# Expert matmuls of a hybrid decoder step: weights as the stationary operand, token blocks of 96 as the moving one

## The chip, the cores and the metric

One core of a Trainium2 chip runs the whole kernel. The metric is device time in microseconds (us) of one execution, median of several; lower is better. Engines are named as in the profile: PE is TensorE's matmul, PEld its loading of the stationary operand, DVE is VectorE, ACT ScalarE, POOL GpSimd, SP the queue that issues the weight transfers.

## The reference

One step of a two-layer decoder for 256 prompt tokens and 8 x 4 sample tokens, 288 rows of width 1024. Layer 0 is a Mamba-2 / sliding-window attention mixer and a dense SwiGLU; layer 1 is an RWKV-7 mixer and a mixture of experts, which is the part that matters here:

```python
def _swiglu(h, wg, wu, wd):
    return (jax.nn.silu(h @ wg) * (h @ wu)) @ wd

def _moe(h, router, wg, wu, wd):                    # 8 experts, D = 1024, EXPERT_FF = 2816
    logits = jnp.einsum('bld,de->ble', h, router)
    top_v, top_i = lax.top_k(logits, 2)
    gates = jax.nn.softmax(top_v, axis=-1)
    combine = jnp.einsum('blk,blke->ble', gates, jax.nn.one_hot(top_i, 8))
    y = jnp.zeros(h.shape, f32)
    for e in range(8):
        y = y + combine[..., e:e + 1] * _swiglu(h, wg[e], wu[e], wd[e])
    return y
```

All values are float32. The 288 rows have 576 (row, expert) pairs. With the reference's own inputs (its default seed) the eight experts get 70, 77, 68, 84, 76, 64, 60 and 77 rows.

## The kernel before, in words

Layer 0 and the RWKV mixer take roughly the first half of the span and are not touched. In the expert part the rows of one expert are gathered into a block of at most 128 slots; a block is one `job(j)`. An expert with more rows than slots gets another block, up to `NJ`. The router's counts decide how many jobs there are, and `jobi` carries the number to every engine; jobs 1 to the last but one run in a hardware loop, job 0 and the last are written out beside it. With the counts above there are eight jobs.

A job walks over 2816 = `FC` x 256 inner columns in `FC` = 11 chunks. For one chunk SP loads 3 MB (`load_part`, L825): 128 x 4096 floats of gate and up weights ("gu") and 128 x 2048 of down weights ("dn"), into a ring of four slots.

The products are wanted to nearly float32 accuracy from single-pass matmuls, so every operand is split in two: a head (ACT rounds it to fp32r, `heads` and `token_heads`, L1418, L1423, L1428) and a rest (DVE subtracts the head from the value, `rests` and `token_rests`, L2143, L2149, L2156). A product is then head x head + head x rest + rest x head, three matmuls that add into the same PSUM bank.

On PE, all matmuls of the helper `mm` stand at L2342. For chunk c the queue has:

- `up(c)`: the tokens are the stationary operand (`hsel`, 128 x 128 for each of the eight k-tiles of D), and the weights stream past as 512 moving columns, gate 256 and up 256. That is 8 x 3 = 24 matmuls. The result has tokens on partitions.
- `down(c - 2)`: 12 matmuls, the activation stationary (`actTm`, tile `actT_split` in the profile) and 512 moving columns of down weights.
- `turn(c - 1)`: since the activation must have inner columns on partitions, two 128 x 128 transposes (L3127) turn it, from PSUM bank 2 or 7.

ACT and DVE make the activation of a chunk from PSUM: Silu of the gate half (ACT, L1486), product with the up half (DVE, L2291), and after the transposes its head (ACT, L1493) and rest (DVE, L2307). Each engine runs its queue strictly in program order. At the end of a job the next block's rows, fetched by POOL from DRAM (`next_rows`), are turned by eight transposes (`turn_tokens`, L3080), and ACT copies the job's result out (`rows_out`, L1435, L1436), which POOL stores. The last job also brings all rows back to their tokens and adds them to the residual.

The lines that matter most in the code are these three, in `up`:

```python
mm(ps[:, c % 2, :], hh[:, k, :], wh[:, k, :], k == 0, False)
mm(ps[:, c % 2, :], hh[:, k, :], wr[:, k, :], False, False)
ins = mm(ps[:, c % 2, :], hr[:, k, :], wh[:, k, :], False, k == KT - 1)
```

(the second argument is the stationary operand, the third the moving one).

Of the kernel before, what the change touches and what calls it, by code (L numbers as in the profile page):

```python
# [5 lines left out]
F32 = mybir.dt.float32  # L6
# [26 lines left out]
FC = FF // 256  # L33
C_DECAY = float(np.exp(-0.5))
# [95 lines left out]
def decoder_trunk(nc, a, out):  # L130
    with ExitStack() as ctx:
# [219 lines left out]
        actTm = [[actTm_[:, (2 * i + u) * 256:(2 * i + u + 1) * 256] for u in range(2)] for i in range(2)]  # L351
# [6 lines left out]
        NJ = NE + 4  # L358
        flags, posn, erow, jrow = [moe_area(16) for _ in range(4)]
        ohx, tmpx = [moe_area(64).rearrange("p (x i) -> p x i", x=4) for _ in range(2)]  # L360
# [11 lines left out]
        DOWN_BANKS = [0, 1, 2, 7, 5, 6, 3, 4]  # L372
        moe_rows = nc.dram_tensor("moe_rows", ((NJ + 1) * P, D), F32, kind="Internal").ap()
        moe_back = nc.dram_tensor("moe_back", (NJ * P, D), F32, kind="Internal").ap()

# [13 lines left out]
        def turned(c):  # L389

            return ps[:, 2 if c % 2 == 0 else 7, 0:256]
# [368 lines left out]
        def _(sp):  # L760
# [110 lines left out]
            jl = sp.value_load(jobi[0:1, 4:5], min_val=NE - 1, max_val=NJ - 1)  # L871
# [12 lines left out]
        def _(pool):  # L884
# [15 lines left out]
            for n, t in enumerate(X_ORDER):  # L900
# [11 lines left out]
                if n == 4:  # L912
                    pool.wait_ge(sem("pool_cleared"), 2)
                    pool.dma_start(moe_rows.rearrange("(b p) n -> p b n", p=P), zeros.unsqueeze(1).broadcast_to([P, NJ + 1, D]))\
                        .then_inc(sem("rows_zeroed"), 16)
                    pool.dma_start(moe_back[(NE - 1) * P:, :].rearrange("(b p) n -> p b n", p=P),
                                   zeros.unsqueeze(1).broadcast_to([P, NJ - NE + 1, D])).then_inc(sem("rows_zeroed"), 16)
# [91 lines left out]
            jl = pool.value_load(jobi[0:1, 4:5], min_val=NE - 1, max_val=NJ - 1)  # L1009
            def next_rows(j):  # L1010
                pool.wait_ge(sem("gather_full"), 2 * j + 2)
                pool.dma_start(xtok, moe_rows[bass.ds(j * P + P, P), :]).then_inc(sem("xtok_loaded"), 16)

            def store_rows(j):
                pool.wait_ge(sem("y_out"), j)
                pool.dma_start(moe_back[bass.ds(j * P - P, P), :], ysb).then_inc(sem("back_stored"), 16)
                pool.wait_ge(sem("back_stored"), 16 * j)
                pool.sem_inc(sem("ysb_free"), 1)

            next_rows(0)  # L1020
            with pool.Fori(1, jl) as j:
                next_rows(j)
                store_rows(j)
            pool.wait_ge(sem("gather_full"), 2 * jl + 2)
            store_rows(jl)
            for c, (t0, n) in enumerate(TOK):
                if c == 2:
                    pool.wait_ge(sem("pair_summed"), 1)
                    pool.wait_ge(sem("y_final"), 2)
                for a_ in range(2):  # L1030
                    pool.indirect_dma_start(pair[a_][c][0:n, :], None, moe_back,
                                            bass.IndirectOffsetOnAxis(ap=rows_in[0:n, 3 * a_ + c:3 * a_ + c + 1], axis=0))\
                        .then_inc(sem(f"pair_loaded{c}"), 16)


        @block.scalar
        def _(act):
# [387 lines left out]
            def token_heads(j, u):  # L1425

                act.wait_ge(sem("gather_full"), 2 * j + 1 + u)
                A(hsel[0][:, 4 * u:4 * u + 4, :], ps[:, 5 + u, :].rearrange("p (k c) -> p k c", k=4), ACT.Copy)\  # L1428
                    .then_inc(sem("hsel_head"), 1)

            def rows_out(j):
# [3 lines left out]
                A(ysb[:, 0:512], ps[:, 3, :], ACT.Copy)  # L1435
                A(ysb[:, 512:1024], ps[:, 4, :], ACT.Copy).then_inc(sem("y_out"), 1)  # L1436
# [29 lines left out]
            def job(j, first, last=False):  # L1466
# [4 lines left out]
                else:  # L1471
                    heads(j, 0, "gu", range(4))
                    rows_out(j)
                    heads(j, 1, "gu", range(2))
                for c in range(FC + 1):
                    if last and c == 5:
                        act.wait_ge(sem("gather_full"), 2 * j + 3)
                        A(sel_last, ps[:, 5, 0:T], ACT.Copy).then_inc(sem("hsel_head"), 1)
                    if last and c in (4, 6, 9):
                        pair_scale((4, 6, 9).index(c))  # L1480
                    if c < FC:
                        act.wait_ge(sem("gu_full"), FC * j + c + 1)
                        act.sem_inc(sem(f"gu_slot_free{c % MS}"), 1)
# [5 lines left out]
                    if c == FC - 1:  # L1489
                        heads(j, c, "dn", range(1))  # L1490
                    if c:
                        act.wait_ge(sem("tr_full"), FC * j + c)
                        A(actTm[(c - 1) % 2][0], turned(c - 1), ACT.Copy).then_inc(sem("tr_head"), 1)  # L1493
                    if c + 2 < FC:
                        heads(j, c + 2, "gu", range(1, 2))
                    if c < FC - 1:
                        heads(j, c, "dn", range(1))
                if last:
                    act.wait_ge(sem("pair_summed"), 2)
                    act.wait_ge(sem("gather_full"), 2 * j + 10)  # L1500
                    A(ysb[:, 0:512], ps[:, 3, :], ACT.Copy).then_inc(sem("y_out"), 1)
# [6 lines left out]
            jl = act.value_load(jobi[0:1, 4:5], min_val=NE - 1, max_val=NJ - 1)  # L1508
# [6 lines left out]
        def _(dve):  # L1515
# [636 lines left out]
            def token_rests(j, u):  # L2152
# [3 lines left out]
                V.tensor_tensor(hsel[1][:, hv, :], ps[:, 5 + u, :].rearrange("p (k c) -> p k c", k=4),  # L2156
# [1126 lines left out]
```

## Time and profile before

| | |
|---|---|
| median of 3 executions | 1634.34 us (1631.61 to 1641.16) |
| the profiled execution, its own time | 1637.31 us |
| its span, first to last instruction | 1634.3 us |
| PE busy / DVE busy / ACT busy | 1590.1 / 1137.9 / 896.8 us |
| mean granted TensorE clock | 0.987 of full |
| matmuls | 10856, and as many loads of a stationary operand |
| HBM read | 379.09 MB, 248 GB/s over the span |

The busy time of PE counts a matmul from its issue to its last result, and neighbours overlap, so a mean of 390 ns is no price of one more matmul; the price is the distance between the starts of neighbours in the timeline. The same holds for PEld.

### The profile page before, as it was taken

To read this page: it belongs to the slowest core of one execution; us is meant where nothing else is said; L and a number is where in the kernel's file an instruction comes from. 1 tells how busy PE (TensorE), PEld (TensorE's weight loads), DVE (VectorE), ACT (ScalarE), POOL (GpSimd) and SP (SyncE) were. 2 spreads that over 40 slices of the span, in tenths; PEclk is the share of its full clock that TensorE was granted. 3 is DMA by queue.
4 is the path that set the end of the run, shared out by engine and by line. 5 is a ranking of instruction groups with operands and counts; after the bars stand their busy time and mean duration, and the time that the engine had idled before them with its cause. 6 is when DMAs were issued, how large, how long until landed. Compare 5 with 4: busy or idle time off the path is not lost.

```text
span 1634.3 us, 27320 instructions
## 1 busy us (share of the span) xinstructions
PE 1590.1 (97%) x10856; PEld 1309.2 (80%) x10856; DVE 1137.9 (70%) x1476; ACT 896.8 (55%) x1190; POOL 123.3 (8%) x180
## 2 busy tenths in 40 slices
PE   9999999999999999899999999999999999999999
PEld 7766687999998777778767878888787887878787
DVE  4663741677766753335468889797988979798897
ACT  3362541544325353343436777676777767687774
POOL 1104000000000003220222000000000000000100
PEclk9999889999999999998999999999999999999999
DMA  8923533544423240000449999797989979798993
GB/s 334 407 94 124 207 130 123 220 187 170 175 81 119 103 155 1 3 3 2 187 165 395 380 376 412 316 427 305 425 350 376 409 312 426 303 425 347 384 423 121
DMA packets 41103, 404.74 MB, mean 248 GB/s; under 512 B 4784, under 2 KB 5072, under 8 KB 11664
## 3 DMA queue, kind: packets, MB, share of 16 engines
q1 hardware_dynamic: 34336, 372.25, 56.6%
q0 software_dynamic: 6672, 31.14, 4.7%
q8 instruction: 70, 1.15, 0.3%
q14 instruction: 25, 0.20, 0.0%
HBM read 379.09 MB, written 26.30 MB: 248 GB/s over the span
## 4 chain that ended last, share of the span: by engine, by line
PE 88%; DVE 5%; ACT 2%; DMA 2%; issue 2%; POOL 0%; DVEq 0%; ACTq 0%; SPq 0%; POOLq 0%
PE ps L2342 85%; DMA ring<-in_moe_w 1%; PE ps L3127 1%; DMA arena<-in_moe_w 1%; DVE rest_ring L2149 1%; PE ps L2809 1%; PE ps L2750 1%; DVE arena L1688 0%; ACT arena L1270 0%; DVE arena L1701 0%; ACT arena L1283 0%; PE ps L3080 0%; PE ps L2544 0%; DVE h L2057 0%; DVE arena L1776 0%
## 5 line engine op out<-in xcount | busy, mean ns | idle before, releaser
L2342 PE MATMUL ps<-head,hsel 128*128 128x512 f32 x1408 | 457.5, 396 | 2.8 <-DVE rest_ring L2149 2.8
L2342 PEld LDWEIGHTS ps<-head,hsel 128*128 128x128 f32 x1408 | 264.3, 188 | 61.5 <-DVE rest_ring L2149 7.8
L2149 DVE TENSOR_TENSOR rest_ring<-ring,head 128x2048 fp32r<-128x2048 f32 x128 | 291.0, 2284 | 14.4 <-ACT head L1423 14.3
L2342 PE MATMUL ps<-arena,ring 128*128 128x288 f32 (+9 forms) x1408 | 256.6, 347 | 1.3 <-ACT arena L1276 1.2
L1423 ACT ACTIVATE head<-ring 128x2048 fp32r<-128x2048 f32 x128 | 243.1, 1912 | 24.9 <-DMA ring<-in_moe_w 24.9
L2342 PEld LDWEIGHTS ps<-arena,ring 128*128 128x128 f32 (+4 forms) x1408 | 199.5, 189 | 53.1 <-issue 7.7
L2342 PE MATMUL ps<-rest_ring,hsel 128*128 128x512 f32 x512 | 199.6, 390 | 0.0
L2342 PE MATMUL ps<-head,actT_split 128*128 128x512 f32 x512 | 169.1, 394 | 9.0 <-issue 6.3
L2342 PE MATMUL ps<-rest_arena,head 128*128 128x288 f32 x704 | 174.8, 296 | 0.0
L2342 PE MATMUL ps<-rest_arena,rest_ring 128*128 128x288 f32 x528 | 155.5, 294 | 0.0
L2342 PE MATMUL ps<-h,ring 128*128 128x288 f32 (+2 forms) x624 | 133.6, 370 | 3.7 <-ACT h L1332 1.9
L2342 PEld LDWEIGHTS ps<-h,ring 128*128 128x128 f32 (+2 forms) x624 | 99.6, 176 | 37.6 <-issue 10.7
L2342 PEld LDWEIGHTS ps<-head,actT_split 128*128 128x128 f32 x512 | 96.1, 188 | 33.3 <-issue 9.1
L2342 PEld LDWEIGHTS ps<-rest_arena,head 128*128 128x128 f32 x704 | 122.5, 188 | 0.1
L2143 DVE TENSOR_TENSOR rest_ring<-ring,head 128x2048 fp32r<-128x2048 f32 x48 | 109.7, 2285 | 9.7 <-ACT head L1418 9.7
L2149 DVE TENSOR_TENSOR rest_arena<-arena,head 128x1024 fp32r<-128x1024 f32 (+1 forms) x64 | 110.3, 1750 | 3.7 <-ACT head L1423 3.5
L2342 PEld LDWEIGHTS ps<-rest_ring,hsel 128*128 128x128 f32 x512 | 96.4, 188 | 18.0
L2342 PE MATMUL ps<-arena 64*64 64x64 f32 (+13 forms) x1514 | 96.9, 266 | 9.9 <-DVE arena L1721 4.0
L2342 PE MATMUL ps<-hsel,head 128*128 128x288 f32 x352 | 103.8, 295 | 0.0
L1599 DVE TENSOR_TENSOR x<-x,ps 128x288 f32<-128x288 f32 x110 | 48.2, 452 | 77.6 <-PE ps L2342 77.3
L1423 ACT ACTIVATE head<-arena 128x1024 fp32r<-128x1024 f32 (+1 forms) x64 | 92.4, 1485 | 15.9 <-DMA arena<-in_moe_w 15.6
L2342 PE MATMUL ps<-rest_ring,actT_split 128*128 128x512 f32 x256 | 99.7, 389 | 0.0
(387 smaller groups left out, 2283.1 us busy)
## 6 DMA issues: line engine op xcount, KB each, us to landing
ring<-in_moe_w SPq DMA_DIRECT2D x64, 2048.0 KB, 12.4
ring<-in_moe_w SPq DMA_DIRECT2D x64, 1024.0 KB, 8.3
arena<-in_moe_w SPq DMA_DIRECT2D x24, 2048.0 KB, 11.6
arena<-in_moe_w SPq DMA_DIRECT2D x24, 1024.0 KB, 6.6
ring<-in_ffn_w SPq DMA_DIRECT2D x11, 2048.0 KB, 7.4
ring<-in_ffn_w SPq DMA_DIRECT2D x11, 1024.0 KB, 4.8
moe_rows<-arena POOLq DMA_DIRECT2D x1, 6656.0 KB, 34.0
ring<-in_w_in SPq DMA_DIRECT2D x2, 3072.0 KB, 12.8
```

Of the source, the lines that this page charges most:

```text
L1423: A(mhead[c % 2][:, o:o + w], mslot[s][:, o:o + w], ACT.Copy).then_inc(sem("gu_head"), 1)
L1599: V.tensor_tensor(x[:, m, :], x[:, m, :], bank(g)[:, 0:T], ALU.add).then_inc(freesem(g), 1)
L2143: V.tensor_tensor(mrest[s][:, GU:SLOT], mslot[s][:, GU:SLOT], down_head(c).bitcast(F32), ALU.subtract).then_inc(sem("dn_split"), 1)
L2149: V.tensor_tensor(mrest[s][:, o:o + w], mslot[s][:, o:o + w], mhead[c % 2][:, o:o + w].bitcast(F32), ALU.subtract).then_inc(sem("gu_split" ...
L2342: return nc.tensor.matmul(o, l, r, start=start, stop=stop, skip_group_check=skip)
L2750: ins = nc.tensor.transpose(b[0:rows, i * P:(i + 1) * P], src[:, 4 * hf + i, t0:t0 + rows], ident)
L2809: ins = nc.tensor.transpose(b[:, n * P:(n + 1) * P], Mi[gg % 2][:, h0:h0 + 2, :].rearrange("p h t -> p (h t)"), ident)
L3127: ins = nc.tensor.transpose(turned(c)[:, u * P:(u + 1) * P], actm[c % 2][:, u * P:(u + 1) * P], ident)
```

## The change

A block has `SL` = 96 slots instead of 128, and up to 13 blocks are foreseen (`NJ`). In `up(c)` the operands change places: each 128 x 128 piece of the gate or up weights is stationary and the tokens stream. The 96 head columns and 96 rest columns of a k-tile lie side by side in `hsel`, so that a piece of the weights' head is loaded once for 192 moving columns (head x head and head x rest), and a piece of the weights' rest once for the 96 head columns. The two sums stand apart in PSUM; ACT copies one to SBUF, DVE adds the other to it, and Silu, product, head and rest are then made of 192 wide tiles in SBUF. The result has inner columns on partitions already, so `turn` is gone. `down` is as before with a 96 wide stationary operand. Two PSUM banks for each of two chunks take the place of one, in banks 0 to 3; down uses 4 and 5, token blocks 6 and 7. POOL's order of loads and stores is written out by chunk, and ACT makes the first piece of the next job's chunk 0 a little earlier. What SP loads is the same.

```diff
+SL = 96
...
-        hsel = [hsel_[:, i * 1024:(i + 1) * 1024].rearrange("p (k c) -> p k c", k=KT) for i in range(2)]
+        hsel = hsel_[:, 0:2 * KT * SL].rearrange("p (k a c) -> p k a c", k=KT, a=2)
...
-        sgm = moe_area(256)
-        actm = [moe_area(256) for _ in range(2)]
+        sgm = [moe_area(2 * SL) for _ in range(2)]
+        gsum = [moe_area(4 * SL) for _ in range(2)]
...
-        NJ = NE + 4
+        NJ = NE + 5
...
-        DOWN_BANKS = [0, 1, 2, 7, 5, 6, 3, 4]
+        GU_BANKS, DOWN, TOKB = (0, 2), 4, 6
+        FINAL_BANKS = [0, 1, 2, 3, 6, 7, 4, 5]
...
-        def turned(c):
-            return ps[:, 2 if c % 2 == 0 else 7, 0:256]
+        def gu_banks(c):
+            b = GU_BANKS[c % 2]
+            return ps[:, b:b + 2, 0:4 * SL].rearrange("p b (i a s) -> p b i a s", i=2, a=2)
+        def sums4(c):
+            return gsum[c % 2].rearrange("p (b i s) -> p b i s", b=2, i=2)
...
+            def act_silu(j, c):
+                act.wait_ge(sem("gu_free"), FC * j + c + 3)
+                A(sgm[c % 2], gsum[c % 2][:, 0:2 * SL], ACT.Silu).then_inc(sem("sums_then_silu"), 1)
+            def act_head(j, c):
+                act.wait_ge(sem("actm_ready"), FC * j + c + 1)
...
+                A(actTm[c % 2][0], sgm[c % 2], ACT.Copy).then_inc(sem("moe_act_head"), 1)
...
-                        act.wait_ge(sem("gu_free"), FC * j + c + 2)
-                        A(sgm, ps[:, c % 2, 0:256], ACT.Silu).then_inc(sem("silu_ready"), 1)
+                    A(sums4(c), gu_banks(c)[:, :, :, 1, :], ACT.Copy).then_inc(sem("sums_then_silu"), 1)
...
-                    if c:
-                        act.wait_ge(sem("tr_full"), FC * j + c)
-                        A(actTm[(c - 1) % 2][0], turned(c - 1), ACT.Copy).then_inc(sem("tr_head"), 1)
+                    act_silu(j, c)
...
+                    if c == FC - 1 and not last:
+                        heads(j + 1, 0, "gu", range(0, 1))
+                    act_head(j, c)
...
+            def act_sums(j, c):
+                dve.wait_ge(sem("sums_then_silu"), 2 * FC * j + 2 * c + 1)
+                V.tensor_tensor(sums4(c), gu_banks(c)[:, :, :, 0, :], sums4(c), ALU.add).then_inc(sem("gu_free"), 1)
+            def act_product(j, c):
+                dve.wait_ge(sem("sums_then_silu"), 2 * FC * j + 2 * c + 2)
+                V.tensor_tensor(sgm[c % 2], sgm[c % 2], gsum[c % 2][:, 2 * SL:4 * SL], ALU.mult).then_inc(sem("actm_ready"), 1)
+            def act_rest(j, c):
+                dve.wait_ge(sem("moe_act_head"), FC * j + c + 1)
+                V.tensor_tensor(actTm[c % 2][1], sgm[c % 2], actTm[c % 2][0].bitcast(F32), ALU.subtract)\
+                    .then_inc(sem("moe_act_rest"), 1)
...
-                        V.tensor_tensor(actm[c % 2], sgm, ps[:, c % 2, 256:512], ALU.mult).then_inc(sem("gu_free"), 1)
...
-                        V.tensor_tensor(hd[1], turned(c - 1), hd[0].bitcast(F32), ALU.subtract).then_inc(sem("tr_free"), 1)
...
                 def up(c):
...
-                        mm(ps[:, c % 2, :], hh[:, k, :], wh[:, k, :], k == 0, False)
-                        mm(ps[:, c % 2, :], hh[:, k, :], wr[:, k, :], False, False)
-                        ins = mm(ps[:, c % 2, :], hr[:, k, :], wh[:, k, :], False, k == KT - 1)
+                        for i in range(4):
+                            cols_ = slice(i * P, (i + 1) * P)
+                            both = sums[:, i // 2, i % 2]
+                            if k == KT - 1:
+                                mm(both[:, 0], wr[:, k, cols_], hsel[:, k, 0, :], False, False, skip=True)
+                            ins = mm(both, wh[:, k, cols_], hsel[:, k], k == 0 and i % 2 == 0, k == KT - 1, skip=True)
+                            if k < KT - 1:
+                                mm(both[:, 0], wr[:, k, cols_], hsel[:, k, 0, :], False, False, skip=True)
...
-                def turn(c):
-                    pe.wait_ge(sem("gu_free"), FC * j + c + 3)
-                    pe.wait_ge(sem("tr_free"), FC * j + c + (1 if c else 2))
-                    for u in range(2):
-                        ins = nc.tensor.transpose(turned(c)[:, u * P:(u + 1) * P], actm[c % 2][:, u * P:(u + 1) * P], ident)
-                    ins.then_inc(sem("tr_full"), 1)
...
-                    pe.wait_ge(sem("tr_free"), FC * j + c + 3)
+                    pe.wait_ge(sem("moe_act_rest"), FC * j + c + 1)
...
-                        mm(ps[:, 3 + hf, :], ah[:, us], wh[:, u, cols_], begins, False)
-                        mm(ps[:, 3 + hf, :], ah[:, us], wr[:, u, cols_], False, False)
-                        ins = mm(ps[:, 3 + hf, :], an[:, us], wh[:, u, cols_], False, ends)
+                        mm(ps[0:SL, DOWN + hf, :], ah[:, us], wh[:, u, cols_], begins, False)
+                        mm(ps[0:SL, DOWN + hf, :], ah[:, us], wr[:, u, cols_], False, False)
+                        ins = mm(ps[0:SL, DOWN + hf, :], an[:, us], wh[:, u, cols_], False, ends)
```


What this makes of PE's queue, at the end of `up(2)`, `down(0)` and the start of `up(3)` in the first written-out job. Before:

```order
L2342 MATMUL ps<-head,actT_split 128x512 x2
L2342 MATMUL ps<-rest_arena,actT_split 128x512
L2342 MATMUL ps<-head,actT_split 128x512
L3127 MATMUL ps<-cst,moe 128x128 x2
L2342 MATMUL ps<-head,hsel 128x512
L2342 MATMUL ps<-rest_ring,hsel 128x512
L2342 MATMUL ps<-head,hsel 128x512 x2
L2342 MATMUL ps<-rest_ring,hsel 128x512
```

and after (the four pieces of a k-tile read alike; `hsel,head` with 192 columns is a weights' head piece, `rest_ring` with 96 a weights' rest piece):

```order
L2377 MATMUL ps<-rest_arena,actT_split 96x512
L2377 MATMUL ps<-head,actT_split 96x512 x2
L2377 MATMUL ps<-rest_arena,actT_split 96x512
L2377 MATMUL ps<-head,actT_split 96x512 x2
L2377 MATMUL ps<-rest_arena,actT_split 96x512
L2377 MATMUL ps<-head,actT_split 96x512
L2377 MATMUL ps<-hsel,head 128x192
L2377 MATMUL ps<-hsel,rest_ring 128x96
L2377 MATMUL ps<-hsel,head 128x192
L2377 MATMUL ps<-hsel,rest_ring 128x96
```

The two transposes between `down` and `up` are gone, `down` has the same matmuls with 96 stationary columns, and a k-tile of `up` has eight matmuls in place of three: 64 in a chunk in place of 24.

DVE's queue, middle of a job (`moe` is the area of the activation tiles, 128x2048 is a rest of the weights). Before:

```order
L2291 TENSOR_TENSOR moe<-moe,ps 128x256
L2143 TENSOR_TENSOR rest_ring<-ring,head 128x2048
L2149 TENSOR_TENSOR rest_arena<-arena,head 128x2048
L2307 TENSOR_TENSOR actT_split<-ps,actT_split 128x256
L2149 TENSOR_TENSOR rest_arena<-arena,head 128x2048
L2291 TENSOR_TENSOR moe<-moe,ps 128x256
```

and after:

```order
L2196 TENSOR_TENSOR moe<-moe 128x192
L2178 TENSOR_TENSOR rest_ring<-ring,head 128x2048
L2201 TENSOR_TENSOR actT_split<-moe,actT_split 128x192
L2178 TENSOR_TENSOR rest_ring<-ring,head 128x2048
L2191 TENSOR_TENSOR moe<-ps,moe 128x384
L2172 TENSOR_TENSOR rest_ring<-ring,head 128x2048
```

The weights' rests keep their number and size; beside them stand three operations of a chunk (384, 192 and 192 wide) in place of two of 256.

## Rows read from the trace of the kernel before

**Rows 1.** The page: busy time; chain that ended last, by engine and by line

```profile
PE 1590.1 (97%) x10856; PEld 1309.2 (80%) x10856; DVE 1137.9 (70%) x1476; ACT 896.8 (55%) x1190; POOL 123.3 (8%) x180
...
PE 88%; DVE 5%; ACT 2%; DMA 2%; issue 2%; POOL 0%; DVEq 0%; ACTq 0%; SPq 0%; POOLq 0%
PE ps L2342 85%; DMA ring<-in_moe_w 1%; PE ps L3127 1%; DMA arena<-in_moe_w 1%; DVE rest_ring L2149 1%; PE ps L2809 1%; PE ps L2750 1%; DVE arena L1688 0%; ACT arena L1270 0%; DVE arena L1701 0%; ACT arena L1283 0%; PE ps L3080 0%; PE ps L2544 0%; DVE h L2057 0%; DVE arena L1776 0%
```

**Rows 2.** Windows: first job; a middle job; six chunks of it; last job; tail

```profile
core 0: us, PE busy (x) PEld busy (x) DVE busy (x) ACT busy (x) POOL busy (x), PEclk, DMA share, GB/s
858.30:954.80 96.50, 94.26 (x427) 77.16 (x427) 80.41 (x86) 65.93 (x58) 12.48 (x8) 1.00 0.91 373
1145.84:1241.44 95.60, 94.41 (x427) 76.94 (x426) 82.40 (x60) 70.25 (x61) 1.07 (x2) 1.00 0.91 373
1175.66:1226.26 50.60, 50.60 (x231) 41.57 (x230) 44.14 (x31) 35.38 (x30) 0.00 (x0) 1.00 0.89 365
1528.74:1617.60 88.86, 87.33 (x398) 70.88 (x397) 83.22 (x66) 65.69 (x55) 12.12 (x7) 1.00 0.84 350
1617.60:1634.30 16.70, 13.56 (x65) 10.57 (x63) 7.92 (x15) 3.44 (x5) 0.00 (x0) 1.00 0.19 71
```

**Rows 3.** Timeline of PE (start us, us, instruction, idle before), chunk of a middle job

```profile
1178.06 0.39 PE L2342 MATMUL ps<-rest_arena,hsel 128*128 128x512 f32 x1
1178.29 0.62 PE L2342 MATMUL ps<-head,hsel 128*128 128x512 f32 x2
1178.74 0.39 PE L2342 MATMUL ps<-rest_arena,hsel 128*128 128x512 f32 x1
...
1181.46 0.39 PE L2342 MATMUL ps<-rest_ring,actT_split 128*128 128x512 f32 x1
1181.69 0.62 PE L2342 MATMUL ps<-third_head,actT_split 128*128 128x512 f32 x2
1182.14 0.39 PE L2342 MATMUL ps<-rest_ring,actT_split 128*128 128x512 f32 x1
```

**Rows 4.** Timeline of PE, token transposes at that job's end

```profile
1234.99 1.04 PE L3080 MATMUL ps<-cst,moe 128*128 128x128 f32 x8
```

**Rows 5.** Timeline of PE, dense layer 0, 288 moving columns

```profile
430.02 0.29 PE L2342 MATMUL ps<-rest_arena,rest_ring 128*128 128x288 f32 x1
430.15 0.29 PE L2342 MATMUL ps<-rest_arena,head 128*128 128x288 f32 x1
430.28 0.29 PE L2342 MATMUL ps<-hsel,head 128*128 128x288 f32 x1
430.42 0.29 PE L2342 MATMUL ps<-rest_arena,rest_ring 128*128 128x288 f32 x1
```

**Rows 6.** Timeline of PEld where the array had stood idle, middle job

```profile
1154.72 0.19 PEld L2342 LDWEIGHTS ps<-head,hsel 128*128 128x128 f32 x1 [0.82 <-DVE rest_ring L2149]
1154.83 0.19 PEld L2342 LDWEIGHTS ps<-rest_ring,hsel 128*128 128x128 f32 x1
```

**Rows 7.** Timeline of PE, same place

```profile
1154.72 0.50 PE L2342 MATMUL ps<-head,hsel 128*128 128x512 f32 x1 [0.40 <-DVE rest_ring L2149]
1155.06 0.40 PE L2342 MATMUL ps<-rest_ring,hsel 128*128 128x512 f32 x1
```

**Rows 8.** Timeline of PEld, 1 moving column, before the experts

```profile
843.30 0.74 PEld L2342 LDWEIGHTS ps<-cst,arena 128*128 128x128 f32 x6 [0.86 <-DVE arena L1543]
```

**Rows 9.** Timeline of PEld, 64 moving columns, RWKV part

```profile
667.53 0.97 PEld L2342 LDWEIGHTS ps<-arena,ring 128*128 128x128 f32 x8
```

**Rows 10.** PEld by form (busy us, mean ns, idle before), widths 128, 64, 32

```profile
L2342 PEld LDWEIGHTS ps<-head,hsel 128*128 128x128 f32 x1408 | 264.3, 188 | 61.5 <-DVE rest_ring L2149 7.8
L2342 PEld LDWEIGHTS ps<-arena,ring 128*128 128x128 f32 x896 | 164.5, 192 | 49.0 <-issue 5.3 <-ACT arena L1276 1.7 <-DVE arena L2092 0.8
...
L2342 PEld LDWEIGHTS ps<-ring 64*64 64x64 f32 x1280 | 26.9, 133 | 17.1 <-issue 17.1
L3127 PEld LDWEIGHTS ps<-cst,moe 128*128 128x128 f32 x176 | 24.1, 140 | 10.4
...
L2342 PEld LDWEIGHTS ps<-ring 32*32 32x32 f32 x96 | 4.0, 107 | 1.6 <-issue 1.5
```

**Rows 11.** Groups of DVE by form, middle job

```profile
L2149 DVE TENSOR_TENSOR rest_ring<-ring,head 128x2048 fp32r<-128x2048 f32 x16 | 36.4, 2284 | 0.5 <-ACT head L1423 0.5
...
L2291 DVE TENSOR_TENSOR moe<-moe,ps 128x256 f32<-128x256 f32 x11 | 4.6, 420 | 8.8 <-ACT moe L1486 8.8
...
L2156 DVE TENSOR_TENSOR hsel<-ps,hsel 128x512 fp32r<-128x512 f32 x2 | 1.3, 682 | 0.0
```

**Rows 12.** Groups of ACT by form, middle job

```profile
L1423 ACT ACTIVATE head<-ring 128x2048 fp32r<-128x2048 f32 x16 | 30.4, 1912 | 1.0 <-DMA ring<-in_moe_w 1.0
...
L1486 ACT ACTIVATE moe<-ps 128x256 f32<-128x256 f32 x11 | 4.2, 385 | 15.7 <-PE ps L2342 15.7
...
L1435 ACT ACTIVATE moe<-ps 128x512 f32<-128x512 f32 x1 | 0.6, 600 | 1.1 <-PE ps L2342 1.1
```

**Rows 13.** Windows: many small matmuls; a stretch with a throttled clock

```profile
680.00:700.00 20.00, 17.87 (x547) 15.74 (x546) 8.05 (x18) 6.33 (x18) 5.10 (x8) 1.00 0.02 5
757.70:771.30 13.60, 13.60 (x106) 10.96 (x103) 7.46 (x13) 5.78 (x15) 0.00 (x0) 0.50 0.00 1
```

More of the change, by code:

```diff
@@ L1008, in _, with pair_rows @@
             pool.wait_ge(sem("jobs_ready"), 1)
-            jl = pool.value_load(jobi[0:1, 4:5], min_val=NE - 1, max_val=NJ - 1)
+            jl = pool.value_load(jobi[0:1, 5:6], min_val=NE - 1, max_val=NJ - 1)
             def next_rows(j):
                 pool.wait_ge(sem("gather_full"), 2 * j + 2)
[L1012 to L1029, printed above, removed]
+                pool.dma_start(xtok[0:SL], moe_rows[bass.ds(j * SL + SL, SL), :]).then_inc(sem("xtok_loaded"), 16)
+            def pair_rows(c):
+                n = TOK[c][1]
                 for a_ in range(2):
@@ L1033, in _, with job @@
                         .then_inc(sem(f"pair_loaded{c}"), 16)
+            def job(j, first, last=False):
+                if not last:
+                    next_rows(j)
+                for c in range(FC):
+                    if c == 0 and not first:
+                        pool.wait_ge(sem("y_out"), j)
+                        pool.dma_start(moe_back[bass.ds(j * SL - SL, SL), :], ysb[0:SL]).then_inc(sem("back_stored"), 16)
+                    if c == 1 and not first:
+                        pool.wait_ge(sem("back_stored"), 16 * j)
+                        pool.wait_ge(sem("gather_full"), 2 * j + 2)
+                        pool.sem_inc(sem("ysb_free"), 1)
+                    if last and c == 1:
+                        pair_rows(0)
+                        pair_rows(1)
+                    if last and c == 7:
+                        pool.wait_ge(sem("pair_summed"), 1)
+                        pool.wait_ge(sem("y_final"), 2)
+                        pair_rows(2)
+            job(0, True)
+            with pool.Fori(1, jl) as j:
+                job(j, False)
+            job(jl, False, last=True)
         @block.scalar
@@ L1500, in job @@
                     act.wait_ge(sem("gather_full"), 2 * j + 10)
-                    A(ysb[:, 0:512], ps[:, 3, :], ACT.Copy).then_inc(sem("y_out"), 1)
+                    A(ysb[0:SL, 0:512], ps[0:SL, DOWN, :], ACT.Copy).then_inc(sem("y_out"), 1)
                     return
@@ L2284, in job @@
                     rests(j, 0, "gu", range(4))
-                    rests(j, 1, "gu", range(0, 1))
-                for c in range(FC + 1):
-                    if c < FC:
-                        dve.wait_ge(sem("silu_ready"), FC * j + c + 1)
-                        if c >= 2:
-                            dve.wait_ge(sem("tr_full"), FC * j + c - 1)
-                        V.tensor_tensor(actm[c % 2], sgm, ps[:, c % 2, 256:512], ALU.mult).then_inc(sem("gu_free"), 1)
+                    rests(j, 1, "gu", range(2))
+                for c in range(FC):
+                    act_sums(j, c)
                     if last and c in (2, 3):
@@ L2297, in job @@
                         pair_add(j, c // 2 - 3, c % 2)
-                    if c == 0 and not first:
-                        rests(j, 1, "gu", range(1, 2))
-                    if 1 <= c <= FC - 2:
+                    if c:
                         rests(j, c - 1, "dn", range(1))
+                    act_product(j, c)
                     if c + 2 < FC:
                         rests(j, c + 2, "gu", range(0, 1))
-                    if c:
-                        dve.wait_ge(sem("tr_head"), FC * j + c)
-                        hd = actTm[(c - 1) % 2]
-                        V.tensor_tensor(hd[1], turned(c - 1), hd[0].bitcast(F32), ALU.subtract).then_inc(sem("tr_free"), 1)
+                    if c == FC - 1:
+                        rests(j, c, "dn", range(1))
+                    act_rest(j, c)
                     if c + 2 < FC:
                         rests(j, c + 2, "gu", range(1, 2))
-                    if c == FC - 2:
-                        rests(j, c, "dn", range(1))
-                rests(j, FC - 1, "dn", range(1))
                 if last:
@@ L3155, in job @@
                         down(c - 2)
-                    if 1 <= c < FC:
-                        turn(c - 1)
                     if c == FC - 1:
-                        turn(c)
                         for u in range(0 if last else 2):
```

110 lines of the change are left out of this document (55 added, 55 removed).

## The prediction

> **What bounds the kernel now.** I read the page first: PE is busy for 97% of the span, and the chain of work that ended last runs for 85% of it over one line, the matmul helper L2342 [rows 1]. Then the windows by stage. The first expert job takes 96.50 us, a middle one 95.60, and six neighbouring chunks of a middle job take 50.60 us, 8.43 us each, with PE busy in all of it, DVE in 44.14 us and ACT in 35.38 [rows 2]. So inside a job PE alone sets the pace.
>
> What a matmul costs PE is read from the distance of starts in the timeline. Three matmuls of 512 moving columns lie between 1178.06 and 1178.74, and between 1181.46 and 1182.14: 0.227 us each, in `up` and in `down` [rows 3]. The eight token transposes last 1.04 us together, one 0.27, so 0.77 / 7 = 0.11 each [rows 4]; the two of `turn` are of the same shape. A chunk is then 36 x 0.227 + 2 x 0.11 = 8.39 us, and 8.43 are seen. With 288 moving columns three matmuls take 0.40 us, 0.133 each [rows 5]. The two prices give a line: 0.42 ns a column (the granted clock is 1.00, the 2.4 GHz level) and 12 ns that do not depend on columns.
>
> Now the other half of an instruction pair, the load of the stationary operand, which today hides under a matmul of 213 ns of streaming. It shows itself where the array had stood idle: after a wait of 0.82 us one load starts at 1154.72 and the next at 1154.83, 0.11 us later [rows 6]; the matmul between them lasts 0.50 us where its neighbours last 0.39 to 0.40 [rows 7], because it had to wait those 0.11 us for its operand. Where the moving side is short, the load is all that is left: six pairs with **one** moving column have loads that span 0.74 us, one 0.19, so 0.55 / 5 = 0.11 us each [rows 8]; eight pairs with 64 moving columns span 0.97 us, 0.78 / 7 = 0.111 each [rows 9]. One and 64 columns cost the same, so the time is the larger of load and stream, not their sum. Those are fp32 operands; whether fp32r loads faster is told by the groups: 188 ns against 192 for a 128 wide load, while 64 wide ones take 133 and 32 wide 107 [rows 10]. Width sets it, and the load of the weights' type is as long as the fp32 one. **A 128 wide load costs about 0.11 us, whatever moves.**
>
> **The change part by part.**
>
> *`up`.* 24 matmuls of 0.227 us, 5.45 us, leave. 64 arrive: 32 with 192 moving columns, 32 with 96. By columns this is less work (9216 in place of 12288), but by the line above they would stream for only 0.092 and 0.052 us, both below the 0.11 of a load, and each of them has a load of its own. I take 0.112 us for each, the value of the rows with short moving sides. 64 x 0.112 = 7.17 us: **+1.72 us a chunk**. The bounds: 0.108, if load follows load as after the idle array (6.91 us), and 0.121, if the 12 ns that fp32r pays between neighbours do not hide and come on top of a load (7.74 us).
>
> *`turn`.* Two transposes leave: -0.22 us a chunk.
>
> *`down`.* Still 12 matmuls of 512 moving columns; a 96 wide load hides as a 128 wide one does. 2.72 us, no change.
>
> Chunk: 8.43 + 1.72 - 0.22 = 9.93 us. 88 chunks (8 jobs x 11): **+132 us**, between +110 and +182.
>
> *DVE.* Before, three rests of 2.28 and two operations of 0.42: 7.7 us. After, three rests (6.85), the 384 wide add, between the 0.42 of 256 and the 0.68 of 512 columns, say 0.55, and two of 192 at no more than 0.42 [rows 11]: at most 8.2 us. *ACT*: three heads of 1.91, a 384 wide copy below the 0.60 of 512, two of 192 below the 0.39 of 256 [rows 12]: at most 7.1 us. Both lie beside 9.93 us of PE and cost nothing. The new chain sums, Silu, product, head, rest must be done one chunk later, since `down(c)` stands behind `up(c + 2)`: five operations of about 2.3 us and two weight rests between them against 7.2 us of `up`. That is cover enough; with a PE chunk under 8.2 us it would not be.
>
> *Waits that go.* A middle job takes 95.60 us: 11 x 8.43 are 92.8, eight token transposes 0.9, and 2 us are waits for rests of the next job's weights and restarts. The first job has 2.9 us of them by the same sum [rows 2]; for the last, whose queue holds other transposes too, I count 2 as for a middle one: 7 x 2 + 2.9 = 17 us. DVE needs 8.2 us for a chunk that takes PE 9.93, so it arrives at the end of a job with a lead. I take 12 of them as gone; 0 to 17 are the bounds. The same slack makes the weight transfers idle more: 3.15 MB in 9.93 us is 317 GB/s where 373 are seen.
>
> *Small things.* Gathering, job ends and token transposes work on 96 in place of 128 columns (a tenth of a microsecond a job); POOL's new order has nothing queued behind it that PE waits for, its loads and stores of rows having most of a job's time. The last rows after the last `up` (16.7 us) [rows 2] keep their twenty-four `down` matmuls. Nothing is put down for these. Layer 0 and RWKV are untouched.
>
> Sum: 132 - 12 = +120 us on the profiled execution's 1637.3 us, 1757; the median of the runs lies 3 us lower, so **1754 us**.
>
> **The rivals.**
>
> *The 12 ns stay on top of every load* (0.121 us): nothing in rows 6 to 9 shows them there, but no row has fp32r operands with a short moving side in a series. +51 us: 1805 us. Chance 15%.
>
> *Loads hide after all, and the change is not slower.* The place is the pair load and matmul in `up`; it decides at 0.089 us a pair, where 64 pairs, 2.72 us of `down` and the 0.04 that 8.43 stands over 8.39 make today's 8.43 again. If loads overlapped each other or were shared by neighbours, the line's 0.092 and 0.052 us would give 4.6 us for `up`, a PE chunk of 7.3, and DVE's 8.2 us would become the bound: 88 x (8.2 - 8.43) = -20, **1614 us**. Against it stand the 0.11 us of rows 6 to 9, for it only that each piece is used once, so that the engine is free to fetch far ahead. The Trainium skill speaks for it: "TensorE: Matmul & The Clock Gate", section on the back-to-back issue gap, has 81 ns as the sustained distance of load and matmul pairs at 128 columns, an estimate of 64 x 0.081 = 5.2 us for `up`, and the same DVE bound. The trace does not agree with that for these types, with 0.11 us at 1 and at 64 columns; the same page's section on weight-path modes gives its fast load only to operands that are not fp32, and whether fp32r counts as such it does not say. Chance 7%.
>
> *PE's clock falls.* In `up` the array would stream for about two thirds of the time (0.144 of 0.224 us by the line). From 757.70 to 771.30 the granted clock was 0.50, the 1.2 GHz level, with PE busy throughout; from 680 to 700, with 547 small matmuls, it stayed at 1.00 [rows 13]. At 1.2 GHz a chunk would take twice its time: +9.9 us each, +290 us if a third of the chunks ran so, 2045 us. Chance 2%.
>
> *More jobs.* If an expert had over 96 rows, a ninth job would cost 11 x 9.93 + 1 = 110 us: 1862 us. The fullest expert has 84. Chance 1%.
>
> **How the numbers follow.** Forecast 75%, then 15, 7, 2 and 1. The forecast's own bounds are 1754 - 22 - 5 = 1727 and, with all waits kept, 1766; the first rival reaches 1805, and 1817 with all waits. I state 1715 to 1815, which leaves out the last three cases, a tenth, and little of the others. Faster by over 0.5% (8 us, about what a measurement of this kernel can tell): 6%, most of the second rival. Within 0.5%: 1%. Slower: 93%.
>
> **What would show it.** Six chunks of a middle job in 59.6 us with PE busy in all of it. Loads in `up` that start 0.11 us apart whether 192 or 96 columns move; 0.12 would be the first rival, 0.07 on the mean the second. A middle job near 110 to 112 us. DVE's busy time in a job about 89 us or less, with gaps that PE's sums end; a DVE without gaps and a PE that waits for rests would prove me wrong. No L3127 rows, granted clock at 1.00, DMA share below 0.8.

## The result and the profile after

| | before | after |
|---|---|---|
| median, beside each other | 1633.47 us (4 runs) | 1896.48 us (4 runs) |
| ratio after / before | | 1.160, 95% interval 1.156 to 1.165 |
| profiled execution, its span | 1634.3 us | 1892.9 us |
| mean granted TensorE clock | 0.987 | 0.920 |

The change costs 263 us. The direction was forecast, and 120 of the 263 us; the measured time lies 81 us above the upper end of the range.

The page of the profile after, three lines of its slices and the line of the queue that fetches instructions; columns are 40 equal slices of the span:

```profile
PE 1836.8 (97%) x14200; PEld 1617.5 (85%) x14200; DVE 1165.6 (62%) x1564; ACT 917.9 (48%) x1278; POOL 117.6 (6%) x180
...
PEclk9999899999999999995999969959959969869999
DMA  8823536353323000436869676667658657756892
...
q8 instruction: 125, 2.05, 0.4%
```

PE is as busy as before [rows 1], and that alone would tell nothing. What is new is the clock line: from the start of the experts (slice 19) it dips again and again, at even distances. The windows say where. First, from the start of `up(0)` in a job to the start of `up(3)`, which is three `up`s and `down(0)`, in this order: a start at full clock, seven chunks inside that job, and the first and last of six starts at half clock with the sum of the six:

```profile
985.86:1010.06 24.20, 24.20 (x206) 23.39 (x205) 21.56 (x18) 17.83 (x18) 0.51 (x1) 1.00 1.01 400
1010.06:1079.36 69.30, 69.30 (x534) 63.63 (x533) 54.37 (x43) 44.01 (x43) 0.00 (x0) 1.00 0.80 317
...
854.94:900.13 45.19, 45.19 (x206) 43.85 (x205) 21.54 (x46) 17.06 (x17) 6.26 (x7) 0.51 0.62 233
...
1642.44:1687.88 45.44, 45.44 (x205) 43.76 (x205) 19.87 (x17) 17.13 (x16) 0.19 (x1) 0.51 0.56 223
sum 271.54, PE 271.54 PEld 262.88 DVE 117.08 ACT 101.03 POOL 6.96; mean PE 45.26 PEld 43.81 DVE 19.51 ACT 16.84 POOL 1.16
```

Seven chunks in 69.30 us are **9.90 us each; the prediction said 9.93**. That part holds. The starts of the loads say the same at full clock; four loads lie between these two, 0.44 / 4 = 0.11 us:

```profile
1020.07 0.19 PEld L2377 LDWEIGHTS ps<-hsel,head 128*128 128x128 f32 x1
...
1020.51 0.19 PEld L2377 LDWEIGHTS ps<-hsel,head 128*128 128x128 f32 x1
```

But a job's start took 24.20 us at full clock and 45 at half, in six of eight jobs: 271.54 - 6 x 24.20 = **126 us**. Where the clock comes back is seen in the start of job 2, cut at the end of its three `up`s and at the rise of the clock:

```profile
1101.04:1142.11 41.07, 41.06 (x192) 41.07 (x193) 14.90 (x12) 12.78 (x12) 0.00 (x0) 0.50 0.60 239
1142.11:1144.67 2.56, 2.56 (x7) 1.67 (x7) 1.70 (x2) 2.23 (x3) 0.00 (x0) 0.50 0.00 0
1144.67:1146.07 1.40, 1.40 (x8) 1.00 (x6) 1.40 (x3) 1.40 (x3) 0.00 (x0) 1.00 0.00 0
```

The three `up`s ran at half clock from end to end, 41.07 us; `down(0)` with its 512 moving columns began at 1142.11, and 2.56 us later the clock was at 1.00. The three `up`s of job 1, begun at 1.00, ran at 1.00 all through.

Second, the ends of jobs, from the start of `up(10)` to the next job's `up(0)`: the one between jobs 0 and 1, the next, and the sum of the six between jobs 0 and 6:

```profile
969.43:985.86 16.43, 16.32 (x109) 13.65 (x108) 9.91 (x12) 11.10 (x13) 0.53 (x1) 1.00 0.60 236
1079.36:1101.04 21.68, 16.50 (x109) 13.46 (x108) 15.16 (x16) 14.19 (x16) 1.01 (x2) 0.98 0.69 252
...
sum 121.40, PE 98.73 PEld 81.02 DVE 82.30 ACT 82.01 POOL 4.89; mean PE 16.46 PEld 13.50 DVE 13.72 ACT 13.67 POOL 0.81
```

Five of them are longer than the first: 121.40 - 6 x 16.43 = **23 us**. The timelines of PE and DVE at such an end name a wait (columns: start, us, instruction, idle before):

```profile
1095.56 0.40 PE L2377 MATMUL ps<-head,actT_split 128*96 128x512 f32 x1
1101.05 0.52 PE L2377 MATMUL ps<-hsel,head 128*128 128x192 f32 x1 [5.09 <-DVE rest_ring L2178]
```

```profile
1093.63 4.62 DVE L2178 TENSOR_TENSOR rest_arena<-arena,head 128x1024 fp32r<-128x1024 f32 x4
1098.17 4.48 DVE L2178 TENSOR_TENSOR rest_ring<-ring,head 128x2048 fp32r<-128x2048 f32 x2
```

The label says DVE. The rows deny it: the first rest that `up(0)` needs is the first of the four from 1093.63, done before the last `down` was. The instructions of the line that closes the loop over jobs (L3199, PE's sequencer) give another reason; beside them the same line before (L3170):

```profile
L3199 PEldq COMPARE_BRANCH  x6: 79/6769/7694, 1093.0 to 1770.8; - x6
```

```profile
L3170 PEldq COMPARE_BRANCH  x6: 83/218/244, 1047.6 to 1526.0; - x6
```

The numbers are minimum, median and maximum in ns; the smallest of each line is the exit from the loop. The five branches back that are taken last 6.2 to 7.7 us, before about 0.22. Queue q8, which fetches instructions, moved one piece during the branch of 1093.0 (window 1093.0:1100.7):

```profile
q8 instruction: 1, 0.02, 0.9%
```

So it did in each of the other four. In the kernel before it moved nothing at all from 1047.5 to 1239.1 us, two rounds of the loop. The total, 2.05 MB against 1.15, would not show this by itself: experiment 6 moves 1.85 MB and has no such wait. Between jobs 0 and 1 no branch is taken, and no time is lost.

The account of the spans, which differ by 1892.9 - 1634.3 = 258.6 us: the experts begin 3.4 us earlier (854.94 against 858.30); low clock 126, branches 23; left are 258.6 + 3.4 - 126 - 23 = 113 us for loads of the stationary operand less waits that went.

### The profile page after: what moved, and what is told of

Read it like the earlier page. It is cut to its first block, busy times and chain, and to the rows that moved or that the text cites. A ratio compares the mean times of both kernels' runs of the same rounds, so it can differ in the third digit from the quotient of the medians.

```text
span 1892.9 us, 34248 instructions
## 1 busy us (share of the span) xinstructions
PE 1836.8 (97%) x14200; PEld 1617.5 (85%) x14200; DVE 1165.6 (62%) x1564; ACT 917.9 (48%) x1278; POOL 117.6 (6%) x180
## 3 DMA queue, kind: packets, MB, share of 16 engines
q8 instruction: 125, 2.05, 0.4%
## 4 chain that ended last, share of the span: by engine, by line
PE 91%; DVE 5%; issue 2%; ACT 2%; POOL 0%; DVEq 0%; ACTq 0%; POOLq 0%
PE ps L2377 89%; DVE rest_arena L2178 1%; DVE rest_ring L2172 1%; PE ps L2844 1%; PE ps L2785 0%; DVE arena L1717 0%; ACT arena L1289 0%; ACT arena L1302 0%; PE ps L2579 0%; DVE arena L1805 0%; DVE arena L1730 0%; DVE rest_ring L2178 0%; DVE h L2086 0%; DVE hsel L2185 0%; POOL ring L950 0%
## 5 line engine op out<-in xcount | busy, mean ns | idle before, releaser
L2377 PE MATMUL ps<-hsel,head 128*128 128x192 f32 (+1 forms) x3168 | 856.4, 346 | 22.0 <-issue 12.0
L2377 PEld LDWEIGHTS ps<-hsel,head 128*128 128x128 f32 x3168 | 684.9, 217 | 28.9 <-issue 24.4
L2377 PE MATMUL ps<-hsel,rest_ring 128*128 128x96 f32 x2048 | 493.4, 251 | 0.0
L2377 PEld LDWEIGHTS ps<-hsel,rest_ring 128*128 128x128 f32 x2048 | 441.6, 218 | 2.0
L2191 DVE TENSOR_TENSOR moe<-ps,moe 128x384 f32<-128x384 f32 x88 | 49.0, 557 | 321.2 <-ACT moe L1514 321.0
L1514 ACT ACTIVATE moe<-ps 128x384 f32<-128x384 f32 x88 | 43.2, 491 | 418.7 <-PE ps L2377 418.7
L2377 PE MATMUL ps<-hsel,rest_arena 128*128 128x96 f32 x768 | 190.0, 258 | 0.0
L2377 PE MATMUL ps<-head,actT_split 128*96 128x512 f32 x512 | 176.6, 409 | 0.9 <-DVE rest_ring L2172 0.2
L2377 PEld LDWEIGHTS ps<-hsel,rest_arena 128*128 128x128 f32 x768 | 171.6, 226 | 0.8
L2377 PEld LDWEIGHTS ps<-head,actT_split 128*96 128x96 f32 x512 | 86.8, 170 | 36.9 <-issue 2.1
```

Source lines behind the costliest of these rows:

```text
L1514: A(sums4(c), gu_banks(c)[:, :, :, 1, :], ACT.Copy).then_inc(sem("sums_then_silu"), 1)
L2191: V.tensor_tensor(sums4(c), gu_banks(c)[:, :, :, 0, :], sums4(c), ALU.add).then_inc(sem("gu_free"), 1)
L2377: return nc.tensor.matmul(o, l, r, start=start, stop=stop, skip_group_check=skip)
```

## The experiments

All change PE's queue alone except where said. Theory A at this point: the loads cost 1.47 us a chunk; the long loop makes PE fetch its code at each branch back and stand empty for 4 to 5 us; there the clock falls to 1.2 GHz and the three `up`s without a `down` between them don't bring it back.

**1. Jobs written out.**

```diff
-            with pe.Fori(1, jl) as j:
-                job(j, False)
+            for j_ in range(1, NE - 1):
+                job(j_, False)
...
+            with pe.If(jl > NE - 1):
+                with pe.Fori(NE - 1, jl) as j:
+                    job(j, False)
```

> PE's queue alone is changed: jobs 1 to 6 are written out one after the other, the loop stays only for a ninth job and later ones. Theory A (the branch back to the loop's start makes PE fetch its instructions anew, PE stands still for 4 to 5 us at five job ends, the granted clock falls there and stays at half for the three `up`s that have no `down` between them): the five waits of about 5 us at job ends and the five stretches of 44 us at half clock go, only the one at the start of job 0 stays; 1896 - 24 - 105 = about 1767 us. Theory B (at job ends PE waits for the rests of the next job's weights from VectorE, as the wait list names them): the waits and the low stretches stay, 1890 to 1900 us. Theory C (the clock falls because the expert stage as a whole, with 96 and 192 moving columns, is too light for it, wherever a job begins): the low stretches stay even without the waits, 1870 us.

Measured: 1789.62 us (ratio to before 1.093, 1.088 to 1.098), 107 less than the change. A middle job, the end before the last job, and the last job's start:

```profile
983.60:1093.50 109.90, 109.80 (x845) 100.66 (x844) 85.87 (x71) 72.68 (x73) 1.01 (x2) 1.00 0.82 323
1626.70:1648.20 21.50, 16.48 (x109) 13.47 (x107) 14.98 (x16) 14.18 (x16) 0.51 (x1) 0.99 0.73 293
1648.20:1693.30 45.10, 45.09 (x204) 43.83 (x205) 18.18 (x18) 16.48 (x16) 3.87 (x4) 0.51 0.63 243
```

The five waits and the five low stretches are gone, and B and C with them: DVE's queue is the same and PE no longer waits for it. What the expectation missed is the new branch before the last job, over the unused loop for further blocks:

```profile
L3201 PEldq COMPARE_BRANCH  x1: 6718/6718/6718, 1641.1 to 1641.1; - x1
```

It is a taken branch again, this time forward, with one piece on q8 during it: 5 us of wait and 21 of low clock, about the 23 us by which 1790 lies over 1767.

**2. Dense matmuls at the start of each job**, loop as in the change:

```diff
+                        if c == 0 and k == 0:
+                            pe.wait_ge(sem("gather_out"), 2 * j + 2)
+                            for _ in range(12):
+                                mm(ps[:, TOKB, :], wh[:, 0, 0:P], wh[:, 0, :], True, True)
```

> The loop as in the change; at the start of `up(0)` of every job 12 matmuls of 512 moving columns are added whose result nobody reads. Theory A with its second half (the clock comes back as soon as dense matmuls run, and the three `up`s of a job's start are what keeps it low): the clock is back some 5 us after `up(0)` begins, each of the six low stretches shrinks from 44 to 51 us to about 8; saved 6 x 18 = 108 us less 12 x 0.227 = 2.7 us for each of 8 jobs: about 1896 - 108 + 22 = 1810 us. If the low stretch has a length of its own, whatever PE runs: 1896 + 6 x 5.3 + 2 x 2.7 = 1933 us. The 5 us waits at job ends stay in both.

Measured: 1811.54 us (1.106, 1.101 to 1.111). The first three `up`s and `down(0)` of job 2, which begin behind the dense matmuls:

```profile
1098.30:1123.60 25.30, 24.53 (x207) 23.69 (x205) 14.79 (x13) 15.38 (x16) 0.00 (x0) 0.99 0.83 334
```

25.30 us in place of 45.03. Work that nobody needs makes the kernel 85 us faster. The clock was low only while the dense matmuls ran, and back just as `up(0)` had begun. So the low stretch has no length of its own; it lasts as long as PE is fed with `up` alone. PE still stands empty for 4 us behind the branch, as expected.

**3. Half the moving columns.** The head matmul of `up` streams 96 columns; the product of the weights' heads with the tokens' rests is left out, and ScalarE reads the heads' sum in its place.

```diff
-                            ins = mm(both, wh[:, k, cols_], hsel[:, k], ...
+                            ins = mm(both[:, 0], wh[:, k, cols_], hsel[:, k, 0, :], ...
```

> The 32 matmuls of `up` with 192 moving columns get 96: the product of the weights' heads with the tokens' rests is left out, and the sum of the heads stands in its place, so 3072 of a chunk's 9216 moving columns go, with all 64 loads kept. If the load of the stationary operand sets the price of a pair (0.112 us): a chunk inside a job stays at 9.90 us, 0.00 to -0.05. If columns counted (0.42 ns each beyond a fixed part): 32 x 96 x 0.42 ns = 1.29 us less, 8.6 us. At half clock the starts of neighbours should come 0.214 us apart for both kinds of matmul. The total may differ from 1896 us only by where the granted clock falls; if fewer columns make the clock fall in more of a job than its first three chunks, it is slower than the change.

Measured: 2116.37 us (one run), 220 us **slower** with a third less to stream. PEld at full clock and at half:

```profile
1061.84 0.19 PEld L2377 LDWEIGHTS ps<-hsel,head 128*128 128x128 f32 x1
...
1062.51 0.19 PEld L2377 LDWEIGHTS ps<-hsel,head 128*128 128x128 f32 x1
```

```profile
1023.87 0.33 PEld L2377 LDWEIGHTS ps<-hsel,head 128*128 128x128 f32 x1
1024.09 0.33 PEld L2377 LDWEIGHTS ps<-hsel,rest_ring 128*128 128x128 f32 x1
1024.30 0.33 PEld L2377 LDWEIGHTS ps<-hsel,head 128*128 128x128 f32 x1
```

Six loads lie between the first two rows: 0.67 / 6 = 0.112 us, at 96 columns just as at 192. At half clock it is 0.21. So the loads, not the columns, set the price of a pair. But with 96 columns the clock did not stay: it moved between its levels all through the experts, and its mean over the span was 0.811 in place of 0.920. Two neighbouring stretches inside a job show it (granted clock before the last two columns); the first holds the end of an `up` and a `down`, the second the `up` behind it:

```profile
1053.90:1060.60 6.70, 6.70 (x25) 5.50 (x25) 2.71 (x3) 3.23 (x4) 0.00 (x0) 0.50 0.56 235
1060.60:1067.40 6.80, 6.80 (x59) 6.54 (x57) 4.99 (x5) 3.28 (x3) 0.00 (x0) 1.00 0.69 258
```

So the expected 9.90 of a whole chunk can't be checked here; the starts of the loads stand in for it.

**4. Written out, dense matmuls in job 0 only.**

> Jobs written out as in e1_written_out, and the 12 dense matmuls at the start of job 0 only. Theory A: clock at 1.00 in the whole expert part but for some 12 us around the start of job 0; e1's time less 20 us, about 1747 us, which is the loads' price alone: 88 chunks of 9.90 in place of 8.43 us, less about 12 us of waits. If the time is above 1765 us, something else than loads, fetches and clock costs time.

Measured: 1783.42 us (1.087, 1.083 to 1.091): 6 us less than experiment 1, not 20, and above the 1765 that the expectation set as a limit. It is above the limit because the last job's start is low again (45.40 us in place of 24.20), behind a branch of 6.1 us, as in experiment 1. And it gains 6 us and not 20 because the clock had fallen already while the tokens were gathered, ahead of the dense matmuls. The gathering took 12.82 us where it took 8.05 in experiment 1, the dense matmuls themselves took 5.0 us at half clock, PE waited 1.3 us before them, and the gathering had begun 5 us later, with more low clock in the stages ahead. Of the 21 us that the low stretch had cost, about 5 are left as a gain. PE's code up to the dense matmuls is the same in both, so when the gathering begins and how long it takes differ from execution to execution:

```profile
849.53 12.82 PE L2377 MATMUL ps<-arena 128*128 128x96 f32 x48 [1.23 <-ACT arena L1485]
```

**5. A gap without a fetch.** As 1, and before `up(0)` PE waits for both rests of chunk 1.

```diff
+                        if c == 0 and k == 0 and not opening:
+                            pe.wait_ge(sem("gu_split"), pieces_to(j, 1, "gu") + 2)
```

> PE's jobs are written out as in e1_written_out (no fetch at the ends of jobs 0 to 5, 1790 us), but before `up(0)` of jobs 1 to 7 PE waits until VectorE has made both rests of chunk 1, some 7 us after the last `down` of the job before. Theory A' (an empty PE of some us followed by three `up`s brings the clock down, whatever PE waits for): the clock falls at every job's start, 44 us each: six more waits of 7 us and six more low stretches that cost 21 us each, 1790 + 6 x 28 = about 1958 us. Rival (only the fetch of instructions does it): the waits alone, 1790 + 6 x 7 = 1832 us, clock at 1.00 at the starts of jobs 1 to 6.

Measured: 1969.78 us (two runs, ratio 1.206). A job's end and the next start:

```profile
1116.40:1139.80 23.40, 16.46 (x109) 13.45 (x108) 16.76 (x16) 14.18 (x16) 1.01 (x2) 0.95 0.72 265
1139.80:1185.60 45.80, 45.78 (x205) 44.19 (x205) 17.17 (x15) 17.13 (x16) 0.00 (x0) 0.51 0.49 198
```

All seven starts behind a wait are low, and the rival is out: an empty PE before three `up`s is enough, whatever it waits for. A wait of 7 us (23.40 - 16.43) costs 22 more (45.80 - 24.20) behind it.

**6. No branch at all in PE's expert part** (eight jobs written out, no loop for a ninth block), dense matmuls in job 0.

> PE's queue has no branch in the expert part (eight jobs written out, none for a ninth block), with the 12 dense matmuls at the start of job 0. In e4_both one low stretch was left, at job 7, behind the branch that steps over the loop for further blocks. Theory A: it goes, with its wait of 5 us and 21 us of low clock: 1783 - 26 = about 1757 us, clock at 1.00 from job 0 to the end. What is then left over 1638 us is the price of the loads alone: 88 x 1.47 = 129 us less about 10 us of waits. Rival (the last job's own work, its pair transposes and gathers, slows its start): 1783 us as before.

Measured: 1763.1 us (1.080, 1.076 to 1.084) for the 1757 expected. The windows are of the profiled execution, which took 1751.36 us at a mean clock of 0.988; the other three took 1759 to 1768 at 0.977 to 0.982, and no trace shows where they lost it. First, a middle and the last job:

```profile
860.90:970.80 109.90, 109.78 (x845) 100.63 (x844) 79.21 (x67) 69.57 (x69) 6.02 (x8) 1.00 0.80 309
1190.70:1300.60 109.90, 109.78 (x845) 100.63 (x844) 85.80 (x71) 72.88 (x73) 1.01 (x2) 1.00 0.81 323
1630.40:1749.70 119.30, 116.16 (x880) 105.23 (x878) 94.77 (x92) 71.16 (x71) 13.52 (x7) 1.00 0.67 271
```

From the first `up` on the clock is at 1.00 throughout, and the rival falls. From the first `up` to the end of the span pass 1749.7 - 860.9 = 888.8 us, before 1634.3 - 858.3 = 776.0: 112.8 us, the 113 of the account found again by another way. A job is 109.90 where it was 95.60 [rows 2]: 11 x 1.47 = 16.2 less the 2 us of waits.

**7. The kernel before with a longer loop.** Two rounds of three written-out jobs in place of six rounds of one.

```diff
-            with pe.Fori(1, jl) as j:
-                job(j, False)
+            with pe.Fori(0, 2) as i_:
+                for d_ in range(3):
+                    job(i_ * 3 + (d_ + 1), False)
```

> The kernel before, with PE's loop over jobs 1 to 6 turned into two rounds of three written-out jobs, so that the loop's body is some three times as long (longer than the body of the change); all else is as before. If a long body is what makes the branch costly: one wait of 4 to 6 us on PE between jobs 3 and 4, its branch record at 4 us or more where the kernel before shows 0.2, and fetches of instructions all along the expert part. Between other jobs nothing. The clock may fall there, but its `up`s stream 512 columns and should bring it back within some 5 us: 1638 + 5 to 10 us. If the branch back costs nothing here: 1638 us, and the wait of the change has another cause.

Measured: 1662.58 us (one run). The branch, and the job end with it after one without (15.16 us):

```profile
L3168 PEldq COMPARE_BRANCH  x2: 76/3312/6547, 1256.8 to 1551.7; - x2
```

```profile
1229.24:1244.40 15.16, 15.16 (x70) 12.43 (x69) 13.03 (x10) 9.22 (x8) 0.00 (x0) 1.00 0.65 251
1244.46:1263.74 19.28, 15.32 (x75) 12.46 (x74) 13.37 (x14) 13.83 (x16) 1.08 (x2) 0.96 0.80 321
1263.74:1278.25 14.51, 13.94 (x51) 10.93 (x51) 6.95 (x5) 6.55 (x5) 0.00 (x0) 0.82 1.02 428
```

The same wait in the kernel before: 6.5 us of branch, 4.1 more for the job end, and a piece on q8 during the branch. The edit also fixes the number of jobs and drops its load ahead of the loop, but neither stands at the branch back; what changed there is the length of the body. The clock fell here too, but the next two `up`s, with 512 columns, lost only 14.51 - 11.89 = 2.6 us where the change loses 21. The other some 20 of the 28 us lie mostly ahead of the loop: the first `up` begins 13 us later than before, 8 of them from stages before the gathering and 5 from the gathering at half clock, and job 0 begins at half clock (0.50 until 876.6 us). Experiment 8 shows that this needs no change of PE's code.

**8. One part alone, in the kernel before:** ScalarE makes the first head of the next job's chunk 0 ahead of its last activation.

```diff
-                    heads(j, 0, "gu", range(4))
+                    heads(j, 0, "gu", range(1, 4))
...
+                    if c == FC and not last:
+                        heads(j + 1, 0, "gu", range(0, 1))
```

> One part of the change alone, put into the kernel before: ScalarE makes the first piece of the next job's chunk 0 before the last activation of a job. The waits at a middle job's end are 2 us of which PE's wait for rests shows 0.4 (middle jobs) as VectorE stays the later of the two: at best 7 x 0.4 = 3 us less, 1635 us; most likely no difference that can be measured.

Measured: 1638.72 against 1634.05 us, ratio 1.002 (0.999 to 1.005): no difference. PE's queue is that of the kernel before, and yet in the profiled execution the clock was low in the gathering ahead of job 0, which took 13.51 us in place of 8.41:

```profile
847.83:861.34 13.51, 13.51 (x48) 10.23 (x48) 5.09 (x3) 5.46 (x4) 0.00 (x0) 0.57 0.88 352
```

None of the experiments is faster than the kernel before; the best form of the change, experiment 6, stands 8% behind it, and it serves no ninth block.

## Why the prediction was right and wrong

- **Price of a load, 0.112 us: right.** 9.90 us a chunk for 9.93, and unmoved by half the columns. The rivals fall: 12 ns on top of each load would have made 10.5, hidden loads 8.2. The Trainium skill's 81 ns for a pair ("TensorE: Matmul & The Clock Gate", back-to-back issue gap) is not reached by fp32r operands with a 128 wide load; the trace shows 112.
- **Waits that go, 12 us: right in kind, 5 us short.** Without branches 109.90 - 11 x 9.90 leaves 1.0 us for a job's end, about what its eight token transposes take, so all of the some 17 went, the upper bound of that term.
- **DVE and ACT beside PE: right.** The 384 wide add takes 0.557 us on the mean (0.55 was put down), and neither engine holds PE up. In a middle job of experiment 6 DVE was busy for 85.8 us (89 or less was said). The DMA share was 0.81 (below 0.8 was said).
- **"The clock falls", 2%: the step that failed.** The prediction counted that the array would stream for two thirds of a pair, and then took one stretch of small matmuls at full clock [rows 13] as a sign that this suffices. It judged the stage as a whole. The place to ask was the start of a job, with three `up`s and no `down` between them, behind whatever pause comes there. There the `up`s kept the clock where they found it: at 1.00 in job 1, at 0.50 for 41 us in job 2, until the matmuls of `down(0)` brought it back. The size was wrong too: 18 of 88 chunks ran their `up` at half clock, not a third. Each lost (41.07 - 21.5) / 3 = 6.5 us and not 9.9, since almost no `down` was among them; the slow beginning of `down(0)` makes up the rest of the 21 us of a start. Rows 13 held a sign against the prediction too: a stretch in which PE was busy for all of 13.60 us and the clock was low throughout.
- **Not among the terms at all: PE's instruction fetch.** 24 matmuls became 64, and the loop's body grew from 427 pairs [rows 2] to 845. The branch back then cost 6 to 8 us of sequencer time and 4 to 5 us of PE, five times, 23 us. Behind each such wait the clock was down, for 21 us more; the sixth low start, of job 0, followed no branch but a gathering in which the clock had fallen. The Trainium skill has the rule: "Runtime: NRT & Kernel Launch", instruction fetch mechanics, says that a taken branch whose target is not in the engine's buffer forces a fetch by DMA before execution goes on. The trace agrees: up to 7.7 us against 0.2, with one piece fetched during each long branch and none in two rounds of the loop before. How large the buffer is no run here fixes; the body with 427 pairs stays in it, those with 845 and with three times 427 do not.
- **The sum.** 120 forecast for loads less waits, 113 found; 23 and 126 us were missing. The direction was right for the reason given, the loads. (One sum of the rivals has a slip: a ninth job would give 1754 + 110 = 1864 us, not 1862; nothing rests on it.)

## What to carry to other kernels

When matmuls of 128 x 128 stationary fp32r operands are made narrower, price the pair by the larger of load and stream, from a place in the trace where the load stands bare. Then count the instructions of the loop's body and look for what PE does directly after each place where it stands empty: here 7 us of wait cost 22 more, because only narrow matmuls followed. And where a wait is labelled with an engine that had long finished, look at the sequencer's branch records.

## What the runs showed of the hardware

- A load of a 128 wide fp32r stationary operand takes 0.112 us from start to start at full clock and 0.21 at half, the same with 96 and with 192 moving columns.
- PE was busy with narrow matmuls for all of 41 us at the 1.2 GHz level and the clock did not rise; 12 matmuls of 512 columns brought it back. The same narrow matmuls, begun at 2.4 GHz, ran there for 21.5 us without a fall.
- Removing a third of the columns of `up`, with all loads kept, made the kernel 220 us slower (one run); the mean granted clock was 0.811 in place of 0.920.
- A taken branch of PE lasted 0.22 us in a loop of 427 pairs, and 6 to 8 us in a loop of 845 or of three times 427, as well as forward over 845 pairs that were not run. PE stood empty for 4 to 5 us behind each of the long ones.
- Why the clock fell in or at the end of the gathering before job 0 in every profiled form of the change, and not in the profile of before, stays open. Experiments 7 and 8 show that it also falls there with the kernel before's own gathering. There it costs about 8 us (an estimate: 5 in the gathering of experiment 8, half of the 5.4 us until the clock is back), since the wide matmuls of job 0 bring it back; in the change it costs a whole low start.
